# A product's scaling on VectorE, cut into one operation per PSUM bank and spread between normalised slices

## What is computed

```python
for l in range(DEPTH_2):
    h = rmsnorm(x, attn_norm[l])
    z = h @ w_in[l]
    (qA, kA, vA, fA, qB, kB, vB, qI, kI, wI, qC, kC, vC, gC, qD, kD, vD, gates) = jnp.split(z, split_at, axis=-1)
    ...
    yB = dsa_attention(rope(heads(qB, DSA_HEADS), pos), rope(kB[:, :, None], pos)[:, :, 0], vB,
                       rope(heads(qI, IDX_HEADS), pos), rope(kI[:, :, None], pos)[:, :, 0], wI)
```

## Time and profile before

| | us |
|---|---|
| median of three timed executions | 3018.77 |
| lowest and highest | 3013.68, 3019.77 |
| the profiled execution, its own time | 3018.43 |
| its span in the trace | 3016.5 |
| TensorE busy in it | 2969.4 (98%) |
| VectorE busy | 1552.5 (51%) |
| ScalarE busy | 1345.6 (45%) |
| GpSimd busy | 1317.5 (44%) |

### The profile page before, as it was taken

How to read it: one execution, slowest core, us unless ns; L and a number is a source line. 1 busy time by engine, 2 the same in 40 slices (tenths; PEclk the granted TensorE clock), 3 DMA queues, 4 the chain that set the end, 5 groups by cost and what they waited for, 6 DMA issues and landing times.

```text
span 3016.5 us, 41506 instructions
## 1 busy us (share of the span) xinstructions
PE 2969.4 (98%) x15950; PEld 2465.0 (82%) x15950; DVE 1552.5 (51%) x2350; ACT 1345.6 (45%) x2268; POOL 1317.5 (44%) x930
## 2 busy tenths in 40 slices
PE   8999999999999999999999999999999999999998
PEld 7778887799988777888888888878787888888887
DVE  7874351497814878672116433167877520273312
ACT  5443344455534446564234443244565533354432
POOL 5336574410254543234455454554332354554543
PEclk9999999999999999999999999999999999999999
DMA  5244333233233422123333332244231233333332
GB/s 159 81 116 139 93 126 96 74 112 112 82 98 93 136 75 82 50 71 98 96 97 95 97 97 95 87 110 137 70 88 43 69 96 98 98 93 97 98 98 71
DMA packets 215042, 288.24 MB, mean 96 GB/s; under 512 B 42698, under 2 KB 122626, under 8 KB 213186
## 3 DMA queue, kind: packets, MB, share of 16 engines
q1 hardware_dynamic: 212354, 280.41, 31.6%
q0 software_dynamic: 880, 2.99, 0.3%
q10 hardware_dynamic: 1616, 2.23, 0.2%
HBM read 270.33 MB, written 4.72 MB: 91 GB/s over the span
## 4 chain that ended last, share of the span: by engine, by line
PE 89%; DVE 6%; ACT 2%; POOL 1%; issue 1%; DMA 0%; SPq 0%; ACTq 0%; DVEq 0%
PE half L866 73%; PE half L1196 2%; PE half L1199 2%; PE half L1198 2%; PE half L1348 2%; PE half L1334 1%; POOL wL L3374 1%; PE half L1405 1%; PE half L1312 1%; DVE arena L2368 1%; PE half L1317 1%; DVE arena L3133 1%; PE half L1121 0%; PE half L1138 0%; DVE rms L2359 0%
## 5 line engine op out<-in xcount | busy, mean ns | idle before, releaser
L3374 POOL TENSOR_TENSOR wL<-slot,wH 128x512 fp32r<-128x512 f32 (+1 forms) x904 | 1285.8, 1431 | 1669.6 <-ACT wH L1515 1668.7
L1515 ACT ACTIVATE wH<-slot 128x512 fp32r<-128x512 f32 (+1 forms) x904 | 558.1, 625 | 1088.4 <-PE half L866 1082.4
L866 PE MATMUL half<-nH,wH 128*128 128x512 f32 x2048 | 809.2, 395 | 5.5 <-POOL wL L3374 2.2
L866 PE MATMUL half<-nH,wL 128*128 128x512 f32 x2048 | 798.1, 390 | 0.0
L866 PE MATMUL half<-nL,wH 128*128 128x512 f32 x2048 | 797.7, 390 | 0.0
L866 PE MATMUL half<-arena_split,wH 128*128 128x512 f32 (+1 forms) x2432 | 736.0, 385 | 1.5 <-issue 1.0
L866 PEld LDWEIGHTS half<-arena_split,wH 128*128 128x128 f32 x2432 | 451.0, 188 | 94.6 <-issue 3.3
L866 PEld LDWEIGHTS half<-nH,wH 128*128 128x128 f32 x2048 | 384.4, 188 | 100.6 <-issue 17.9
L866 PE MATMUL half<-arena_split,wL 128*128 128x512 f32 (+1 forms) x1216 | 466.4, 384 | 0.0
L866 PEld LDWEIGHTS half<-nH,wL 128*128 128x128 f32 x2048 | 384.4, 188 | 81.7
L866 PEld LDWEIGHTS half<-nL,wH 128*128 128x128 f32 x2048 | 384.7, 188 | 78.2 <-issue 1.4
(11 more groups left out here) (403 smaller groups left out, 3654.4 us busy)
## 6 DMA issues: line engine op xcount, KB each, us to landing
slot<-in_w_in SPq DMA_DIRECT2D x344, 256.0 KB, 2.7
slot<-in_w_up SPq DMA_DIRECT2D x400, 128.0 KB, 2.2
slot<-in_w_down SPq DMA_DIRECT2D x132, 256.0 KB, 2.7
slot<-in_w_branch SPq DMA_DIRECT2D x64, 256.0 KB, 2.7
slot<-in_w_out SPq DMA_DIRECT2D x48, 256.0 KB, 2.8
arena<-arena SPq DMA_DIRECT2D x40, 256.0 KB, 4.4
slot<-in_w_gate SPq DMA_DIRECT2D x48, 128.0 KB, 2.4
arena<-in_w_gate SPq DMA_DIRECT2D x40, 128.0 KB, 2.4
```

Of the source, the lines that this page charges most:

```text
L866: mm = pe.matmul(dst, lhsT, rhs, start=(k == 0 and m == 0), stop=(k == last and m == 2))
L1515: act.activation(wH[:, p, 0:cols], slot[:, s, 0:cols], ACT.Copy).then_inc(weights_high, 1)
L3374: pool.tensor_tensor(wL[:, p, 0:cols], slot[:, s, 0:cols], plainly(wH[:, p, 0:cols]), ALU.subtract)\
```

## The change

`split_norm` takes a table from slice numbers to functions in place of one function and one number. For `bmix1` the one 128x2048 multiplication behind slice 3 becomes four of 128x512: bank 0 behind slice 2, bank 1 behind slice 3, bank 2 behind slice 4 and bank 3 behind slice 5. The wait for `bmix1` stands before the first, and the release of half 0 hangs on the last.

```diff
-            def split_norm(name, gains, l=0, ks=range(KD), between=None, at=1):
+            def split_norm(name, gains, l=0, ks=range(KD), between={}):
...
                     if k + 2 in ks:
                         whole_chunk(k + 2)
-                    if between and k == at:
-                        between()
+                    if k in between:
+                        between[k]()
...
-            split_norm("ass_ff", gains, between=scaled_up_a)
+            split_norm("ass_ff", gains, between={1: scaled_up_a})
...
-                def scaled_mix():
+                def scaled_mix(c):
 
-                    done(dve, "bmix1", l)
                     h = jobs.half["bmix1"]
-                    dve.tensor_tensor(mix1, banks(h), all_rms(NB), ALU.mult).then_inc(drained[h], 1)
+                    if c == 0:
+                        done(dve, "bmix1", l)
+                    ins = dve.tensor_tensor(mix1[:, c, :], banks(h)[:, c, :], rms[:, :], ALU.mult)
+                    if c == NB - 1:
+                        ins.then_inc(drained[h], 1)
+
+                pieces_of_mix = {2 + c: lambda c=c: scaled_mix(c) for c in range(NB)}
...
-                    split_norm("bss_at", both, l, between=scaled_mix, at=3)
+                    split_norm("bss_at", both, l, between=pieces_of_mix)
...
-                    split_norm("bss_at", vec[:, W_AT:W_AT + KD], l, between=scaled_mix, at=3)
+                    split_norm("bss_at", vec[:, W_AT:W_AT + KD], l, between=pieces_of_mix)
...
-                split_norm("bss_ff", gains, l, between=scaled_up_b)
+                split_norm("bss_ff", gains, l, between={1: scaled_up_b})
```

## The result

The changed kernel took 3026.59 us (median of 8 runs, 3024.27 to 3028.75) against 3017.52 for the kernel before (8 runs, 3013.68 to 3021.84): a ratio of 1.0031 with a 95% interval of 1.0022 to 1.0039. It is **slower by 0.3%**, where +0.12% and a range up to 3026.0 were forecast. The profiled execution has its own time of 3024.86 us and a span of 3023.1, 6.6 above before; it is the second fastest of the eight.

A forecast was written before the change was run, and what follows sets the result against it. TensorE was taken to bound nearly all of the kernel. Index products 1.8 us later plus one clock drop of 1.7 gave +3.5 us on 3018.43, so 3021.9 us (+0.12%), range 3017.8 to 3026.0.

The forecast's parts named there:

- The second path: From the bmix1 scaling's end through partner transfers, turn and key copies to the index products; slack 1.3 us in layer 0, none in layer 1.
- the wait for the key copies: At TensorE's index products: over 2 us in both layers, 2.2 and 2.7 us long, with the products 1.8 us later in total.
- what `bmix2` gains turns into idle time there: TensorE arrives at the index products at 985.2 in layer 0, so all bmix2 won is spent waiting.
- From the scaling's end to the turn's start were 6.9 us; I keep that.: Partner transfers before the turn: duration unchanged in both layers, so the turn starts at 977.2 and 2008.4.
- I count one drop in the two layers at 1.7 us.: Clock falls behind TensorE's idle time at the index products: one costing 1.7 us, with none and two as bounds.
- The release: Last scaling piece on VectorE, freeing half 0: complete at 970.26, 2.3 us later than before.
- Pieces: The 128x512 scalings on VectorE: about 0.68 us each, four making 2.72 us against 2.28 for the single operation.
- `bmix2` ended 1.24 us earlier: TensorE in bmix2: forecast to end 1.5 us earlier, with gaps of about 0.4, 0.5 and 1.0 us replacing one of 1.7.
- The turn: VectorE's three operations after the transfers: two lengthened beside GpSimd, 2.28 + 3.27 + 3.27 plus 0.05 between, 8.9 us.
- Rival 3: Transfers or weight rests drag on, the turn stays as hindered, the whole delay arrives: +6.8, 3025.2 us; chance 0.20.
- Rival 2: Units 4 and 5 miss the turn, which is freed of GpSimd and takes 6.9 us: -2.1, 3016.3 us; chance 0.12.
- Rival 1: The clock still falls in bmix2 despite smaller gaps, and no drop follows at the index products: +1.8, 3020.2 us; chance 0.20.

## Why the prediction was wrong

**The place and the kind were right.** The second path was named, the wait for the key copies in both layers was forecast, with the point that what `bmix2` gains turns into idle time there. The three runs that move one thing each (cut 0.9997, moved 1.0022, release alone 1.0013) bear it out, and so does the cover that removes the loss.

**The size failed in three terms of the sum**, all in the same direction. It was +3.5 us; the two measurements gave +9.1 and +5.6.

1. *"From the scaling's end to the turn's start were 6.9 us; I keep that."* This is the step that failed most. In layer 0 it became 8.5 (980.26 less 971.78) and was 8.4 to 8.5 in every kernel with a late release and the loads behind it, but 6.9 in the kernels with an early one. Layer 1 of the changed kernel had 6.9, less than the 7.5 of the profile before, which the forecast carried over there. So the duration read in one execution and one layer held in neither place. With it, layer 0's index products came 2.55 us later in place of 0.65 (1.55 of the difference by this term, 0.35 by the third); layer 1 had 1.03 in place of 1.2. Together 3.6 for the forecast 1.8.
2. *"I count one drop in the two layers at 1.7 us."* Two profiles of the change show one fall through 6 us of matmuls and two through 3.4 us each: some 3 us lost in either execution. The size of one fall was taken right, their number or length by half. The idle time ahead of the fall was 3.7 us in layer 0, longer than the 2.2 of the forecast because of the first term; behind idle times of that length the clock fell in all three profiles that had one (the change twice, the move alone).
3. *The release.* 2.3 us were forecast, 2.65 measured: whole slice 6 took 1.10 us beside an operation of GpSimd (POOL's rest of weights at 968.10), where 0.74 was counted.

Terms 1 and 3 together made 3.6 in place of 1.8 and term 2 some 3 in place of 1.7: 6.6 us, as much as the two profiled spans differ by (the 1.18 ahead of the place and the 1.05 behind it nearly cancel). The executions' own times differ by 6.4. The other 2.6 us of the +9.1 lie between these two executions and the medians of their kernels (1.7 above the one of the change, 0.9 below the one before) and no profile explains them; in part they are chance, as +5.6 was measured the second time.

The steps in between held. Pieces were 0.68; `bmix2` ended 1.24 us earlier for the forecast 1.5, with gaps of 0.25, 0.66 and 0.69 for 0.4, 0.5 and 1.0 (by the prediction's own numbers the first would have been 0.26: 967.27 less the end of unit 3, 968.69 - 1.68). The turn took 2.29, 3.26 and 3.26 for 2.28, 3.27 and 3.27. One step toward that was not as told: unit 4 was rounded at 979.5 (980.68 less 1.18) and not near 977.4, as ScalarE waited 3.4 us for its load. The turn had moved about as far, so it met two of GpSimd's operations all the same. This part is in some measure luck.

The Trainium skill (SBUF — State Buffer, Who interferes with whom) calls the shared ports an exclusive lock. The trace agrees: GpSimd's rest of unit 4, issued while VectorE worked, ended 1.15 us behind VectorE's operation (983.70 against 982.55), and VectorE's next one took 0.97 us longer than the one before:

```profile
981.39 2.31 POOL L3379 TENSOR_TENSOR wL<-slot,wH 128x512 fp32r<-128x512 f32 x1 [2.50 <-ACT wH L1515]
```

**The rivals.** Rival 3, the other side, gave 3025.2 us and was nearest in size, with another cause: it named transfers that drag on, but as a way to a turn hindered three times; the turn was hindered twice, and what grew in layer 0 was the transfer ahead of it. That it came so near in size is luck. Rival 2 didn't come. Rival 1, a fall of the clock inside `bmix2` in spite of the smaller gaps, is real but rarer than with the large gap: of the layers profiled, 3 of 14 with the pieces spread (none of the four of the change itself) and 6 of 12 with one gap of 1.7 to 1.9 us. The three lie in layer 1. What the range missed was that its uncertain terms lean on each other: a later turn makes a longer idle time, and behind the longest ones (3.7 to 3.8 us) the clock fell each time.

## What to carry to other kernels

When an operation is cut and spread, follow its last piece first: what hung on the whole result now hangs on that piece, and here the bounding engine had 1.3 us of slack on that path in one layer and none in the other. A DMA on a path that is shifted has to be priced again, with a bound for another duration (here 6.9 to 8.5 us for the same four transfers), not carried over. If the schedule ahead of a wait gets faster, put more independent work ahead of the wait in the same change: one more unit of weights here turned +0.2 to +0.3% into about -0.08%, the first clear of noise, the second not.

## What the runs showed of the hardware

The gap of TensorE inside `bmix2`, 1.7 to 1.9 us, was followed by the lower clock in 6 of 12 cases, waits at the index products of 2.1 to 2.2 us in 1 of 4, and the two of 1.7 and 1.8 us there (only the release late) in none. Elsewhere in the same thirteen executions a gap of 2.0 us near 641 us was followed by it in 11 of 13, and waits of 1.9 us in the attention (near 1160 and 2195 us) in 8 of 12. So below 2.3 us the length of a gap doesn't tell whether the clock falls. The same program thus differs by some 1.7 us per place from run to run, and its profiles can't be compared without a look at the granted clock.

The longer transfer in layer 0 goes together with one packet on an instruction queue. In the changed kernel it starts 4.9 us behind the release, while the last partner transfer is under way (issues from 974 to 978 us, with time to landing):

```profile
q8 instruction: 1, 0.02, 2.1%
...
arena<-arena SPq DMA_DIRECT2D x1, 256.0 KB, 6.5
```

In layer 0 with the early release the same packet came some 7 us behind it, when the transfers had landed (before, the cut alone, one unit more on the kernel before: 6.9 us); with the late one it came 4 to 5 us behind it (the change twice, the move, the late release, one unit more, the keys first: 8.4 to 8.5 us). With nothing else in the queue and the packet in the middle, 7.8 us were needed. In layer 1 no kernel had it among the transfers, and they took 6.9 us with the early and with the late release (7.5 once, in the profile before). The packet itself took 1.3 us of one engine (2.1% of 16 in 4 us), near the 1.6 us that were added; in the second execution of the change it took 0.9, and as much was added. That it causes the longer transfer wasn't tried, and stays open.
